# The first expert's turn in two halves, with its weight buffers refilled from the middle of it

## The reference, cut to what matters

```python
hg = jnp.einsum('bld,edf->blef', u, p['moe_w_gate'][l])     # 16 experts, 1024 x 512 each
hu = jnp.einsum('bld,edf->blef', u, p['moe_w_up'][l])
h = jax.nn.silu(hg) * hu * gates.astype(u.dtype)[..., None]
return jnp.einsum('blef,efd->bld', h, p['moe_w_down'][l])   # 512 x 1024 each
```

## Time and profile before

| | |
|---|---|
| median of 3 runs | 1223.74 us (1223.24 to 1226.55) |
| the profiled execution | 1224.85 us, its span 1223.0 us |
| TensorE busy | 1114.9 us, 91% of the span |
| VectorE, ScalarE, GpSimd busy | 389.9, 233.9, 140.8 us |
| mean granted clock of TensorE | 0.966 of full speed |
| moved by DMA | 338.24 MB, 277 GB/s over the span |
| chain that ended last | TensorE 68%, DMA 18%, VectorE 7% |
| its largest transfer | up weights of the experts, 12% |

### The profile page before, as it was taken

The page is one execution under the profiler, slowest core; times in us unless marked ns, Lnnn a source line. Parts: engine busy times, 40 slices in busy tenths (PEclk is TensorE's granted clock), DMA queues, the critical chain, the costliest instruction groups (busy, mean ns, idle before and its releaser), DMA issues.

```text
span 1223.0 us, 23538 instructions
## 1 busy us (share of the span) xinstructions
PE 1114.9 (91%) x10201; PEld 622.1 (51%) x10201; DVE 389.9 (32%) x1023; ACT 233.9 (19%) x501; POOL 140.8 (12%) x163
## 2 busy tenths in 40 slices
PE   5899999899989959988889999999998995998986
PEld 3443445555575535545455555545666553555543
DVE  3201331574251300111233633587624230101104
ACT  2002201321231111101053232321012111111112
POOL 1043100022120000000010000042232000000001
PEclk9999999999989989999999999999998998999998
DMA  9998755359559998999996202002395999899994
GB/s 385 398 304 288 312 206 209 145 174 406 200 233 336 405 386 331 371 395 417 416 324 209 73 16 69 1 1 69 153 360 218 367 407 383 324 374 398 406 419 176
DMA packets 73018, 338.24 MB, mean 277 GB/s; under 512 B 6740, under 2 KB 16243, under 8 KB 58128
## 3 DMA queue, kind: packets, MB, share of 16 engines
q1 hardware_dynamic: 60760, 299.14, 63.2%
q0 software_dynamic: 10864, 36.42, 8.6%
q10 hardware_dynamic: 1288, 1.14, 0.3%
HBM read 314.24 MB, written 22.44 MB: 275 GB/s over the span
## 4 chain that ended last, share of the span: by engine, by line
PE 68%; DMA 18%; DVE 7%; issue 2%; ACT 2%; SPq 1%; POOL 1%; ACTq 0%; DVEq 0%; POOLq 0%
PE ps L2359 16%; DMA ring<-in_moe_w_up 12%; PE ps L1987 11%; PE ps L2562 10%; PE ps L2065 8%; PE ps L2383 7%; PE ps L2622 3%; DMA ring<-in_rec_w_in 3%; PE ps L2008 2%; PE ps L2292 2%; PE ps L2592 1%; PE ps L2342 1%; PE ps L2369 1%; PE ps L1980 1%; ACT work L1183 1%
## 5 line engine op out<-in xcount | busy, mean ns | idle before, releaser
L2359 PE MATMUL ps<-ring,work 128*32 128x256 f32 x4736 | 295.8, 394 | 53.4 <-DMA ring<-in_moe_w_up 49.3
L2359 PEld LDWEIGHTS ps<-ring,work 128*32 128x32 f32 x4736 | 150.4, 113 | 152.4 <-issue 66.3
L2562 PE MATMUL ps<-uT,ring 128*128 128x386 f32 x384 | 128.8, 488 | 0.9 <-issue 0.9
L2383 PE MATMUL ps<-ring,work 128*32 128x256 f32 x1728 | 103.0, 380 | 2.1 <-DVE work L1814 2.1
L2562 PEld LDWEIGHTS ps<-uT,ring 128*128 128x128 f32 x384 | 71.7, 190 | 49.6 <-issue 2.4
L1814 DVE COPY work<-ps 128x128 f32<-128x128 f32 x74 | 21.5, 291 | 235.4 <-PE ps L2369 234.3
L2065 PE MATMUL ps<-uT,ring 128*128 128x384 f32 x256 | 89.2, 505 | 3.0 <-DMA ring<-in_rec_w_in 1.9
L1195 ACT ACTIVATE work<-ps 128x128 f32<-128x128 f32 x74 | 20.5, 277 | 337.0 <-PE ps L2359 337.0
L1987 PE MATMUL ps<-ring,uT 128*128 128x512 f32 x192 | 84.1, 595 | 0.0
L2383 PEld LDWEIGHTS ps<-ring,work 128*32 128x32 f32 x1728 | 55.8, 110 | 39.8 <-DVE work L1814 3.0
L1810 DVE TENSOR_TENSOR work<-ps,work 128x128 f32<-128x128 f32 x74 | 21.6, 292 | 155.6 <-ACT work L1195 155.6
(11 more groups left out here) (371 smaller groups left out, 1194.9 us busy)
## 6 DMA issues: line engine op xcount, KB each, us to landing
ring<-in_moe_w_gate SPq DMA_DIRECT2D x32, 2048.0 KB, 12.8
ring<-in_moe_w_up SPq DMA_DIRECT2D x32, 2048.0 KB, 18.0
ring<-in_ada_w SPq DMA_DIRECT2D x24, 2048.0 KB, 11.3
ring<-in_moe_w_down SPq DMA_DIRECT2D x22, 2048.0 KB, 24.1
uT<-in_moe_w_down SPq DMA_DIRECT2D x10, 1536.0 KB, 16.4
ring<-in_rec_w_in SPq DMA_DIRECT2D x6, 2048.0 KB, 23.5
ring<-in_hy_w_in SPq DMA_DIRECT2D x6, 2048.0 KB, 13.4
y_rows<-work SPq DMA_DIRECT2D x64, 96.0 KB, 12.7
```

Of the source, the lines that this page charges most:

```text
L2359: ins = pe.matmul(bank(key)[32 * q:32 * q + 32, 0:2 * P].rearrange("p (a n) -> p a n", a=2), xg[:, u, k, 32 * i:32 * i + 32], ring[:, 3 * ...
L2383: ins = pe.matmul(bank(key)[32 * q:32 * q + 32, 0:256], hT[:, (FIRST[p] + i) % 2, 32 * k:32 * k + 32], w[:, q * 256:(q + 1) * 256], start= ...
L2562: ins = pe.matmul(bank(key)[:, 0:T + 2], w[:, k, (m % 4) * P:(m % 4 + 1) * P], uH[:, k, :], start=(k == 0), stop=(k == DC - 1))
```

## The change

Four things change together.

1. Turn 0 runs the first half of the features for all three tiles, then the second half for all three. Its three tiles now need three PSUM banks at once (0, 1 and 5).
2. At the end of the first halves TensorE signals `half_spent`. SyncE then loads steps 0 to 3 of gate and up of turn 2 into the half of slots 0 and 1 that came free. The waits for the gathered rows and for the whole of turn 0 stand behind these loads, and steps 4 to 7 follow them.
3. In layer 1, steps 0 to 2 of turn 2's gate and up are loaded before the turns begin into `early`, in the place where `x_tok` lies later. From the middle of turn 0 come steps 3 to 6, behind the waits only step 7. TensorE takes the first three steps of turn 2 from `early`.
4. Three semaphores at the start of the kernel are merged into one (`rec_small_cleared`); GpSimd clears these areas in the same order as before.

```diff
@@ claim_moe
+                if p == 0:
+                    for i, b in enumerate((0, 1, 5)):
+                        claim((l, p, "GU", i), b)
                 for i in range(TILES[p]):
                     par = (FIRST[p] + i) % 2
-                    claim((l, p, "GU", i), par)
+                    if p:
+                        claim((l, p, "GU", i), par)
@@ buffers
+        EARLY = 3
+        early = work[:, 12288:12288 + 2 * EARLY * DE].rearrange("p (a n) -> p a n", a=2)
@@ moe_loads
+                def load_rows(kind, e, ks, at):
+
+                    n = ks.stop - ks.start
+                    sp.dma_start(ring[:, kind, at * DE:(at + n) * DE].rearrange("p (k n) -> p k n", k=n),
+                                 moe_src(l, kind, e)[:, ks, :]).then_inc(S(f"slot{kind}_loaded"), 16)
+
...
-                    full(sp, (l, p, "GU", TILES[p] - 1))
                     if p == 0:
+                        sp.wait_ge(S("half_spent"), l + 1)
+                        for kind in range(2):
+                            load_rows(kind, e, slice(EARLY * l, 4 + EARLY * l), 0)
                         sp.wait_ge(S("rows1_loaded"), 16 * (l * (NE // 2) + 1))
                         sp.wait_ge(S("rows0_loaded"), 16 * (l * (NE // 2 - 1) + 1))
-                    load_part(0, e, u)
-                    load_part(1, e, u)
+                        full(sp, (l, p, "GU", TILES[p] - 1))
+                        for kind in range(2):
+                            load_rows(kind, e, slice(4 + EARLY * l, 8), 4)
+                    else:
+                        full(sp, (l, p, "GU", TILES[p] - 1))
+                        load_part(0, e, u)
+                        load_part(1, e, u)
...
                     load_extra(2)
+                    for kind in range(2):
+                        sp.dma_start(early[:, kind, :].rearrange("p (k n) -> p k n", k=EARLY),
+                                     moe_src(l, kind, 2)[:, 0:EARLY, :]).then_inc(S("early_loaded"), 16)
@@ ScalarE, turn 0
                 for i in range(TILES[0]):
+                    if i >= 2:
+                        evacuated(act, (l, 0, "GU", i - 2))
                     silu(0, i)
@@ TensorE, gate_up
+                            if l == 1 and p == 2:
+                                pe.wait_ge(S("early_loaded"), 32)
...
+                            w = ring[:, 3 * u:3 * u + 2, at:at + P]
+                            if l == 1 and p == 2:
+                                w = early[:, :, at:at + P] if k < EARLY else ring[:, 0:2, at - EARLY * DE:at - EARLY * DE + P]
...
                     if half == 1:
                         done(ins, key)
+                    elif p == 0 and i == TILES[0] - 1:
+                        ins.then_inc(S("half_spent"), 1)
@@ TensorE, turn 0
-                both_halves(0, 0)
-                both_halves(0, 1)
+                for half in range(2):
+                    for i in range(TILES[0]):
+                        gate_up(0, i, half)
                 hidden_t(0, 0)
-                both_halves(0, 2)
                 hidden_t(0, 1)
                 down(0, 0)
                 down(0, 1)
```

More of the change, by code:

```diff
@@ L419, in add_moe @@
             for s in range(RING):
-                slot_uses[s] += {2: 6, 5: 5}.get(s, NE // 2)
+                slot_uses[s] += {0: NE // 2 + 1, 1: NE // 2 + 1, 2: 6, 5: 5}.get(s, NE // 2)
         moe_base = {}
@@ L790, in clear @@
                 pool.memset(ap, 0.0).then_inc(S(name), 1)
-            clear(wg, "wg_cleared")
+            clear(wg, "rec_small_cleared")
             clear(zeros[:], "zeros_cleared")
-            clear(gkw, "gkw_cleared")
+            clear(gkw, "rec_small_cleared")
             clear(g36, "g36_cleared")
-            clear(mcol, "mcol_cleared")
+            clear(mcol, "rec_small_cleared")
             pool.memset(vb[:, :, :, DV:DV + 1], 1.0).then_inc(S("vb_ones"), 1)
             pool.wait_ge(S("slot2_loaded"), 32)
-            pool.wait_ge(S("wg_cleared"), 1)
+            pool.wait_ge(S("rec_small_cleared"), 1)
             w_in = A["rec_w_in"][0].rearrange("(k p) n -> p k n", p=P)
@@ L807, in _ @@
                                w_in[:, :, base + 8 * d + 4 * typ:base + 8 * d + 4 * typ + 4]).then_inc(S("wg_loaded"), 16)
-            pool.wait_ge(S("gkw_cleared"), 1)
+            pool.wait_ge(S("rec_small_cleared"), 2)
             for d in range(2):
                 pool.dma_start(gkw[16 * d:16 * d + 16, 256 * d:256 * d + 256], A["gla_gk_w"][0, d]).then_inc(S("rec_small_loaded"), 16)
-            pool.wait_ge(S("mcol_cleared"), 1)
+            pool.wait_ge(S("rec_small_cleared"), 3)
             for d in range(2):
@@ L1389, in _ @@
             full(v, "gk")
-            v.wait_ge(S("gkw_cleared"), 1)
+            v.wait_ge(S("rec_small_cleared"), 2)
             free(v.tensor_copy(gkT, bank("gk")[0:32, 0:T]), "gk")
@@ L2352, in gate_up @@
                                 evacuated(pe, (l, p, "X", h))
+                            if l == 1 and p == 2:
+                                pe.wait_ge(S("early_loaded"), 32)
                             for n in range(3 * u, 3 * u + 2):
-                                pe.wait_ge(S(f"slot{n}_loaded"), 16 * (base[n] + 1 + p // 2))
+                                pe.wait_ge(S(f"slot{n}_loaded"), 16 * (base[n] + 1 + p // 2 + (1 if u == 0 and p else 0)))
                         opened(pe, key)
@@ L2358, in gate_up @@
                             at = k * DE + q * P
+                            w = ring[:, 3 * u:3 * u + 2, at:at + P]
+                            if l == 1 and p == 2:
+                                w = early[:, :, at:at + P] if k < EARLY else ring[:, 0:2, at - EARLY * DE:at - EARLY * DE + P]
                             ins = pe.matmul(bank(key)[32 * q:32 * q + 32, 0:2 * P].rearrange("p (a n) -> p a n", a=2),
-                                            xg[:, u, k, 32 * i:32 * i + 32], ring[:, 3 * u:3 * u + 2, at:at + P],
+                                            xg[:, u, k, 32 * i:32 * i + 32], w,
                                             start=(k == 0), stop=(k == DC - 1))
```

## The result

The changed kernel takes 1240.19 us in the median (1236.17 to 1245.19) against 1223.49 us for the kernel before in the same job: 1.015 times as long, 95% interval 1.0121 to 1.0179. The forecast was 1224.4 us in a range of 1220.5 to 1228.5, so it was wrong.

The account below looks back on a forecast made before the run. TensorE paces turns 1 to 5, the weight stream from turn 6 on. Layer 0: 2.1 - 2.0 = +0.1 us; layer 1: 2.2 - 1.6 = +0.6 us; 1223.74 + 0.7 = 1224.4 us, range 1220.5 to 1228.5.

Parts of the forecast that it names:

- What bounds the kernel: Expert turns of both layers: TensorE sets the pace in turns 1 to 5, the weight stream from turn 6 on.
- The cap on the gain: Stall of turn 6: gain at most the smallest queue, 2.0 us in layer 0 and 1.6 us in layer 1.
- the price of the meeting: Before turn 1: early loads share engines with the last scatters, rows 2.1 us late in layer 0, 2.2 us in layer 1.
- The alternation piece by piece: Scatter beside half loads: queues alternate by pieces whatever their size, so the scatter keeps a third, 0.133 MB per us.
- my 0.40 MB: Layer 0, when the loads flow: 0.27 MB of scatters left plus 0.13 MB displaced, taking 3.0 us.
- The clock: TensorE after idling before turn 1: lower clock would cost 1.6 us more each layer, kept only for the range.
- The slow one: Rival, before turn 1: rows 4.1 and 4.7 us late, clock lost in both layers, +8.4 us, 1232.1 us; chance 0.12.
- a fifth of the rate: Slow rival's mechanism: the scatter gets 0.08 MB per us beside the loads, its bytes taking 5.0 and 6.5 us.
- pieces are not cut to 4 KB: Half loads travel in 8 KB pieces; the rival with 4 KB pieces gave delays 1.1 and 1.0 us, 1222.2 us; chance 0.08.
- The whole advance: Rival, turns 3 to 5: deeper queues, all 14.1 us of moved bytes count, -9.8 us, 1213.9 us; chance 0.05.
- no collision: Rival, before turn 1: scatters through or served before the loads flow, -2.9 us, 1220.8 us; chance 0.15.
- Turn 0 and the rest: Turn 0's order costs TensorE 0.4 to 0.8 us, covered by late rows; second load parts hidden, merged semaphores 0.

Follow-up runs that it names:

- e2: The change, but SyncE waits for the six scatters to land before it issues the half loads; 1235.45 us, ratio 1.0102.
- e10: The change, but SyncE issues the gather of turns 1 and 2 once the scatters landed, half loads right behind in its queue; 1226.57 us, ratio 1.002.
- e4: The change, but GpSimd issues the half loads in its own queue, behind its last scatter and ahead of the gather; 1232.04 us, ratio 1.0064.
- e3: e1 plus the 1.57 MB of turn 2's weights loaded ahead of the turns in layer 1; 1222.85 us, ratio 0.9996.
- e9: The kernel before with its old turn 0, plus only the 1.57 MB loaded ahead of the turns in layer 1; 1221.22 us, ratio 0.9991.
- e1: The change with only turn 0's new order: both load parts behind the waits, no early steps in layer 1; 1224.94 us, ratio 1.0023.
- e6: The change with only the gate half load issued from the middle of turn 0, the up half behind the waits; 1235.38 us, ratio 1.0103.
- e8: The change with each early half load cut into two transfers of two steps, pieces of 4 KB; 1235.48 us, ratio 1.0093.

## Why the prediction was wrong

**What bounds the kernel** was read rightly. Turns 1 to 5 are paced by TensorE, and a shift of turn 1 by 3 us or more went through to the stall of turn 6 in every experiment.

**The cap on the gain** held as an upper bound. 2.10 and 3.67 MB were moved forward. After turn 1 the gate loads found 0.9 and 1.4 us of queue before them (they land in 8.8 and 9.3 us, had 11.6 and 11.3), after turn 2 in layer 0 none (7.9 us). Turn 6's loads were issued 9.3 and 6.0 us late and the last of them landed 8.3 and 5.6 us late: a gain of 1.0 and 0.4 us where I had 2.0 and 1.6, and not the 5.1 and 9.0 us of the moved bytes. (The load at 1001.0 us in the earlier trace rows, which the prediction puts after turn 4, is the one after turn 3; the sum does not change by it.)

**The failed step is the price of the meeting**, "2.1 us late" and "2.2 us late"; turn 1 was 6.1 and 4.4 us late. The alternation piece by piece that I took from the earlier trace rows is real, and stands in the trace from 367 us on. I applied it from the first microsecond of the loads. In its place the scatter first gets next to nothing for about 3 us in layer 0 and 2 us in layer 1, and then its share. It also had more left than my 0.40 MB: 0.54 MB at 364 us, 2.7 us after the issue of the loads. The last scatter so landed 11.9 us after its issue, where my sum gives about 7.1. That it is the meeting of the queues is shown by e2 against e10 (a gather of 9.6 us beside the loads, of 3.9 us ahead of them in their own queue) and borne out by e4; e10 shows that it is nearly all of the loss. The trace of before had a sign that I did not weigh: the third gather, issued at 370.56 us between the two loads of turn 2, took 12.0 us to land.

```profile
370.56 0.51 POOL L918 DMA_DIRECT2D work<-x_rows  x1 [4.73 <-PE ps L2342]
...
work<-x_rows POOLq DMA_DIRECT2D x1, 384.0 KB, 12.0
```

**The clock** was the second, smaller miss. I named 1.6 us for each layer, and left it out of the sum because the idle time was to be under 2.1 us. With 6.1 and 4.7 us of waiting it was lost in both: from turn 1's transposes to the loads after turn 1 it is 21.1 and 20.1 us in the place of 18.2, 2.9 and 1.9 us. The reason for leaving it out was not sound either: in e10 the clock fell behind waits of 1.1 and 1.3 us, in e3 and e9 it did not behind 2.0 and 1.8 us.

**The sum by its terms**, layer 0: late rows 6.1 (2.1), clock and the like 2.9 (0), a remainder of 0.3, gain -1.0 (-2.0), together 8.3 (0.1). Layer 1: 4.4 (2.2), 1.9 (0), -0.3, -0.4 (-1.6), together 5.6 (0.6).

**The rivals.** The slow one gave 1232.1 us, with delays of 4.1 and 4.7 us and the clock lost twice; its chance of 0.12 was far too low. Its mechanism, a fifth of the rate, is not what the trace shows; the delay in layer 1 came near, and its total of 8.4 us is half of what was measured. That pieces are not cut to 4 KB is confirmed: 36 pieces of q1 carry 0.29 MB, 8 KB each. The Trainium skill's preferred packet of at most 4096 B ("DMA: Bandwidth & Descriptors", section "SWDGE vs HWDGE vs iDMA") does not describe these loads. The whole advance, and no collision, fell.

**Turn 0 and the rest.** The changed order cost 0.1 us up to the end of turn 0 and was covered, as forecast; alone (e1) it is at most 0.4%. The early steps ahead of the turns cost nothing.

**What stays open** is why GpSimd's queue is silent when SyncE's loads begin. The silence was about 1, 1 to 2, 2 to 3 and 5 us with pieces of 2, 4, 8 and 16 KB, and did not appear where the gather was issued 0.4 us before the loads. Pieces already handed to the engines ahead of its turn would fit; nothing here shows them. Open too is the size of the delay beyond the silence. It was larger in the two layers where the loads were issued more than a microsecond ahead of the last scatter (e6, layer 1: 4.5 against 3.3 us; e8, layer 0: 8.3 against 3.7 us), which no run varied by itself.

## What to carry to other kernels

As far as these runs show, moving a load forward is worth no more than the shortest queue that stands before any later load whose release does not move with it; read that queue from landing times, against the landing of the same load on idle engines. Before loads are moved beside a small transfer of another queue that the critical engine waits for, look in the trace for a place where this pair already meets, and take the whole landing time from there, not the share of the rate. And a wait that no data need may be the one that keeps two queues apart: here, leaving it out cost 1.4%.

## What the runs showed of the hardware

- A transfer of GpSimd's queue whose data did not flow yet when SyncE's loads began got next to nothing (1 piece in a microsecond, against 36) for 2 to 3 us beside pieces of 8 KB, then alternated one for one.
- The same gather took 5.9 us when issued 0.4 us before the loads, 11.5 us when issued 1.2 us behind them.
- In one queue a scatter with 2.1 MB of loads behind it landed in 4.8 us, as fast as alone.
- A wait of 1.09 us, with the 0.70 us wait that follows the transposes, was followed by the lower level of the granted clock in e10 (32 matmuls in 3.48 us). Waits of 2.01 us in e3 and 1.81 us in e9, each with the same 0.70 us, were not (PEclk 1.00, 1.93 us). What decides between the two is not shown.
